# Expert weights of a fused decoder trunk: gate and up blocks loaded as one transfer each

## What is computed

```
def expert_block(args):
    xblk, e = args
    hid = jax.nn.silu(xblk @ w_gate[e]) * (xblk @ w_up[e])
    return hid @ w_down[e]
```

## Time and profile before

| | |
|---|---|
| median of three runs | 1823.66 us (1822.59 to 1826.57) |
| the profiled execution | 1824.36 us, of which the traced span is 1822.3 us |
| PE, DVE, ACT busy | 97%, 72%, 57% of the span |
| HBM read, written | 484.66 MB, 26.74 MB |
| expert loads | 3 x 128 DMAs of 1 MB, 10.9 to 11.7 us from issue to landing (medians) |

### The profile page before, as it was taken

One profiled execution on the slowest core, in us unless ns is written; L12 is line 12 of the kernel. 1 busy time (PEld: TensorE's weight loads), 2 busy tenths in 40 slices (PEclk: granted clock), 3 DMA queues, 4 the chain that ended last, 5 costly groups with the idle time before them and its releaser, 6 DMA issues.

```text
span 1822.3 us, 21866 instructions
## 1 busy us (share of the span) xinstructions
PE 1767.5 (97%) x7712; PEld 1183.5 (65%) x7719; DVE 1315.4 (72%) x1368; ACT 1030.0 (57%) x1067; POOL 227.2 (12%) x136
## 2 busy tenths in 40 slices
PE   8999998999999999999999999998999999999997
PEld 6876785566555555657787777877565555555564
DVE  4999757888778878864443533456878888888877
ACT  4225636777777777753221312233777777777774
POOL 0030001112221222100000000000021222221220
PEclk9999999999999999989999999999999999999999
DMA  8521046999999999994212221222899999999995
GB/s 281 185 93 47 13 176 242 402 409 402 404 400 397 394 399 397 395 368 153 83 57 93 93 93 46 93 93 93 316 408 408 408 401 398 407 402 398 400 389 232
DMA packets 101503, 494.95 MB, mean 272 GB/s; under 512 B 14153, under 2 KB 26441, under 8 KB 52160
## 3 DMA queue, kind: packets, MB, share of 16 engines
q1 hardware_dynamic: 88192, 467.69, 65.7%
q0 software_dynamic: 10176, 16.24, 2.7%
q10 hardware_dynamic: 3072, 10.18, 1.5%
HBM read 484.66 MB, written 26.74 MB: 281 GB/s over the span
## 4 chain that ended last, share of the span: by engine, by line
PE 51%; DMA 28%; DVE 12%; ACT 6%; issue 2%; SPq 1%; DVEq 0%; ACTq 0%
DMA raw<-in_expert_w_gate 28%; PE psum L901 8%; PE psum L902 8%; PE psum L903 8%; DVE w_lo L729 6%; ACT w_hi L742 5%; PE psum L1050 4%; PE psum L984 4%; PE psum L981 3%; PE psum L1434 2%; DVE xs L1918 2%; PE psum L1060 1%; PE psum L1065 1%; PE psum L1061 1%; PE psum L1002 1%
## 5 line engine op out<-in xcount | busy, mean ns | idle before, releaser
L729 DVE TENSOR_TENSOR w_lo<-raw,w_hi 128x2048 fp32r<-128x2048 f32 x320 | 731.5, 2288 | 181.5 <-ACT w_hi L742 175.3
L742 ACT ACTIVATE w_hi<-raw 128x2048 fp32r<-128x2048 f32 x320 | 610.8, 1912 | 229.0 <-DMA raw<-in_expert_w_up 116.5
L984 PE MATMUL psum<-w_lo,uT_hi 128*64 128x512 f32 x992 | 273.4, 397 | 5.8 <-DVE w_lo L729 2.3
L707 ACT ACTIVATE w_hi<-raw 128x2048 fp32r<-128x2048 f32 x46 | 88.0, 1914 | 329.7 <-PE psum L903 329.6
L981 PE MATMUL psum<-w_hi,uT_hi 128*128 128x512 f32 x868 | 248.7, 403 | 6.6 <-DVE uT_hi L2191 6.6
L715 DVE TENSOR_TENSOR w_lo<-raw,w_hi 128x2048 fp32r<-128x2048 f32 x46 | 105.4, 2291 | 200.2 <-ACT w_hi L707 200.2
L2521 POOL DMA_INDIRECT y_dram<-y_e,index x60 | 137.5, 2292 | 786.3 <-DVE y_e L2226 773.1
L1050 PE MATMUL psum<-raw,hidT_f 128*64 128x512 f32 (+1 forms) x496 | 226.1, 598 | 0.0
L984 PEld LDWEIGHTS psum<-w_lo,uT_hi 128*64 128x64 f32 x992 | 130.4, 135 | 103.6 <-DVE w_lo L729 26.9
L981 PEld LDWEIGHTS psum<-w_hi,uT_hi 128*128 128x128 f32 x868 | 161.6, 192 | 45.3 <-DVE uT_hi L2191 7.2
L2516 POOL DMA_INDIRECT x_e<-xs_dram,index x64 | 73.3, 1145 | 672.3 <-DVE index L2186 625.8
(11 more groups left out here) (267 smaller groups left out, 2348.6 us busy)
## 6 DMA issues: line engine op xcount, KB each, us to landing
raw<-in_expert_w_gate SPq DMA_DIRECT2D x128, 1024.0 KB, 11.5
raw<-in_expert_w_up SPq DMA_DIRECT2D x128, 1024.0 KB, 11.7
raw<-in_expert_w_down SPq DMA_DIRECT2D x128, 1024.0 KB, 10.9
raw<-in_odd_w_in SPq DMA_DIRECT2D x8, 2048.0 KB, 9.6
raw<-in_odd_w_in SPq DMA_DIRECT2D x8, 1024.0 KB, 7.9
raw<-in_odd_w_out SPq DMA_DIRECT2D x4, 2048.0 KB, 7.5
raw<-in_even_w_in SPq DMA_DIRECT2D x3, 2048.0 KB, 12.5
y_dram<-zeros SPq DMA_DIRECT2D x8, 512.0 KB, 12.5
```

The costliest lines, as they stand in the source:

```text
L729: nc.vector.tensor_tensor(part(w_lo[b]), src, part(w_hi[b]).bitcast(F32), ALU.subtract).then_inc(m.lo[b], 1)
L742: nc.scalar.activation(part(w_hi[b]), src, ACT.Copy).then_inc(m.hi[b], 1)
L984: mm = nc.tensor.matmul(psum[0:FIRST, bank], xeT_hi[:, 8 * b + 4 * half + j, 0:FIRST], lo[:, j], start=False, stop=False)
```

## The change

Gate and up blocks are loaded by one DMA each, with 16 KB in each partition, by the new function load_block. It waits for the second half of the slot only (the first half has been split by then, as DVE splits in order), and adds to `landed`. Down is loaded in halves as before. ACT waits for the whole block before it splits either half of gate or up. `front_at` now counts down blocks alone. Nothing is changed in what the engines compute or in their order.

```diff
+    def down_block(n):
+
+        k = n - moe_start[int(n >= moe_start[1])]
+        return k == n_moe - 1 or k >= 2 and (k - 2) % 3 == 2
+
...
         front_at[n] = 16 * sum(1 for e in list(range(moe_start[0], first_odd)) + list(range(moe_start[1], n + 1))
-                               if e <= n and e % SLOTS == n % SLOTS)
+                               if e <= n and e % SLOTS == n % SLOTS and down_block(e))
...
-                if raw_half:
+                if raw_half or not is_down(k):
                     eng.wait_ge(landed[n % SLOTS], landed_at[n] + 32 * turn)
                 else:
                     eng.wait_ge(front[n % SLOTS], front_at[n] + 32 * turn)
...
                         if s or kind != "down":
-                            for half in range(2):
-                                load_half(kind, number, x, turn, half)
+                            if kind == "down":
+                                for half in range(2):
+                                    load_half(kind, number, x, turn, half)
+                            else:
+                                load_block(kind, number, x, turn)
...
+                def load_block(kind, s, e, turn):
+
+                    src, number = {"gate": (wg_dram, gate_no), "up": (wu_dram, up_no)}[kind]
+                    n = first + number(s)
+                    freed(n - SLOTS, 1, turn)
+                    sp.dma_start(raw[:, n % SLOTS], one(src, layer, e)).then_inc(landed[n % SLOTS], 16)
```

## The result

| | before | after |
|---|---|---|
| median | 1823.12 us (1821.6 to 1827.03, six runs) | 1846.26 us (1838.07 to 1849.58, six runs) |
| ratio to before | | 1.0114, interval 1.0099 to 1.0129 |
| profiled execution | 1824.36 us | 1838.07 us, its fastest |

The changed kernel is slower by 1.1%. I had forecast no change. Some executions of any of these kernels run a few per cent slower throughout, at a lower clock; they are left out of all ratios. The profiled execution of after is 13.7 us longer than that of before, and this is the difference that the traces can explain.

What follows compares the result with a forecast made beforehand. The prediction took DMA as the full engine pacing the expert parts. A shorter stream, later start and later splits summed to -7.8 + 3.3 + 4.6 = +0.1 us, so no change: median 1823.8 us, range 1815 to 1834.

Steps and rivals of the forecast that it cites:

- What bounds the kernel: Expert parts: DMA is full from the start; PE waits each step for the last split of up and for `uT_lo`.
- Term 1: Weight load stream in the experts: 16 KB rows save 0.075 us a block over 52 blocks x 2 layers, -7.8 us.
- rival 2: Load queue: 16 KB rows are cut into two packets, so term 1 shrinks to 0.8 us; +7.1, 1831 us; chance 0.08.
- The faster stretches: Sign in the load stream: a stretch with gate and up alone should read about 428 GB/s.
- Term 2: Start of each layer's experts: first gate load goes out only when the whole block can, 2.3 us later; +3.3 us together.
- Term 3: PE's last wait in each layer: weights of a landed block are split 2.3 us later, +4.6 us together.
- Does the DMA stay fed?: Check on load issue in expert steps: each load goes out 2.6 us before the one ahead lands; all fits, narrowly.
- with 1.3 to spare: Gate load in an expert step: out 3.9 us before down's second half lands, 1.3 us beyond the 2.6 needed.
- The 2.6 us themselves: Lead a load needs: 5.1 us from issue to landing of a half in idle queues, of which 2.5 are data.
- Rival 1: Second layer, 26 steps: up issued too late, needing 3.5 us of lead, engines dry 0.4 us each; +10, 1834; chance 0.15.
- Rivals 3 and 4: Expert steps get shorter: long rows lessen the loss beside gathers, 1807 us, chance 0.12; or fewer transfers, 1795, chance 0.04.
- rival 4: Expert steps: each transfer holds the engines a fixed time; two fewer leave PE's 15.7 us pace; 1795 us; chance 0.04.

Runs made afterwards that it cites:

- e15: Kernel before, SP's loop written out, first gate load of each step held until down's first half landed; two runs, 1843.56 and 1850.71 us.
- e1: Kernel before with the changed kernel's late issue and late split of gate and up, but 8 KB rows; two runs, 1840.37 and 1845.73 us.
- after again: The changed kernel measured a second time, beside the follow-up runs; ratio 1.0068 to before, +12.4 us.
- e2: Kernel before, but ACT waits for the whole gate or up block before splitting, halves issued as before; ratio 1.0035 to before, +6.4 us.
- e3: Kernel before, but both halves of gate or up issued together when the second is free, split as they land; ratio 0.9982 to before, -3.3 us.
- e9: Changed kernel with gather and scatter of each expert step cut to one 4 KB row; ratio 1.0272 to before, +75 us to before with the same cut.
- e13: Control: kernel before with SP's loop over the steps written out, same loads, order and waits; 1827.24 us, ratio 1.0003 to before.
- e14: Kernel before, SP's loop written out, first gate load of each step held until the up block ahead landed; 1818.47 us, ratio 0.9952 to before.

## Why the prediction was wrong, point by point

- **What bounds the kernel.** Right: DMA with the waits of PE at the line that takes `uT_lo`.
- **Term 1, -7.8 us.** Its price was right, its arrival not. Packets of the load queue in 1320 to 1740 fell by a third, and they are of 16 KB, so rival 2 fell:

```profile
q1 hardware_dynamic: 14669, 160.80, 95.9%
```

  The same row of before has 22403 packets. A clean stretch, 1233.5 to 1237, has 79 packets of 16 KB beside 15 tiny ones; 86.4% x 3.5 us x 16 / 79 = 612 ns, against 618 to 624 expected and 2 x 309. But from the first gate load inside the experts to the one behind PE's last wait, the stream got 2.2 us longer in the first layer and 3.4 in the second, where 3.9 less were due in each. The steps are 16.45 us, not 16.05. The faster stretches, which I had named as a sign, are there (the best of 40 slices of 1320 to 1740 reads 427 GB/s, in before 423), but didn't show in the steps: the table above says why.
- **Term 2, +3.3 us.** Right. Against the time at which the second half of its buffer is free, the first gate load of the experts lands 2.8 us later in the first layer and 1.0 in the second, where its second half had been slow in before too (7.1 us from issue to landing, 5.7 in the first layer): 3.8 together. That the gathers would take some of it back is not shown.
- **Term 3, +4.6 us.** Right. At its last wait PE ran 2.5 us further behind the landings in either layer, 4.9 together. In one step the last split of up ended 6.5 us after the landing that ACT waited for, as forecast (times, DVE; ACT began at 1578.33):

```profile
1580.29 4.49 DVE L734 TENSOR_TENSOR w_lo<-raw,w_hi 128x2048 fp32r<-128x2048 f32 x2 [0.55 <-ACT w_hi L747]
```

- **"Does the DMA stay fed?"** This is the step that failed. It asked whether each load goes out 2.6 us before the one ahead has landed. It did: gate was out 3.6 to 3.9 us ahead, up 4.0. But it took the landings of the step as given, at the old pace, and so measured spare time against a point that the loads themselves move. The question was whether a buffer gets round in a step: 7.3 us from landing to split, which was right, plus SP's 0.4, which I had left out, plus the 7.9 us of a load into idle queues, 15.6 of the 16.05 that I had forecast for a step. My sentence "with 1.3 to spare" held for the lead and hid that under 0.5 us was left for the queue, of which a gate load took 0.86. The rows for it stood there: the earlier trace rows.
- **The 2.6 us themselves.** They came from one load into idle queues, and say when the first packets flow, not when the last of 16 engines has work. e15 cost three times what they give. The Trainium skill, page "DMA: Bandwidth & Descriptors", section "Why a DMA increments its semaphore by 16 and not by 1", says that the engines of a DMA finish independently and each adds its own 1. The trace agrees: those 16 come 5.1 us apart on average in before, and up to 8.3. A landing is the last engine's, and the others need their next work earlier.
- **Rivals.** Rival 1 named the right place and sign, at 1834 us; the median was 1846. By it the step would have gone from 16.2 to 16.6 us, and in the second layer only. In fact the first layer lost too, as its steps at 15.7 us were gone from the start: the loop binds PE-bound steps as well. Rivals 3 and 4 fell: no step got shorter. To rival 4, the fixed time per transfer: e1, with two transfers for each of after's, is 2 to 7 us slower than after again (two runs), where 32 us had been at stake.
- **The new sum.** In the profiled pair: +5.6 for the stream in place of -7.8, +3.8 and +4.9 for terms 2 and 3, and 2.9 us at the end of the first layer, where the last scatter landed later. Against that stands -3.4 before the first expert part, in work that the change doesn't touch. These are pieces of one shift, one behind the other, and make +13.8, as much as the two spans differ (1822.3 and 1836.1). The median of the six runs is 8 us above the profiled one; of this no trace tells.

## What to carry to other kernels

Before merging loads into bigger ones, go once round each buffer: issue to landing in idle queues, landing to the last reader, and the issue itself. If the sum comes near the step, every wait in the queue lengthens the step, however far ahead the load seems to go out. A merged load makes both parts of the loop longer at once, and either alone may be free (e2, e3) where the pair is not (e1). Where a queue is kept very full, try to hold one load back: at one place it was worth 9 us here, at all three it cost 7.

## What the hardware showed that I had not expected

- A load into idle queues reaches its first engine 0.95 to 1.0 us after the issue and its last of 16 after 1.8 to 2.3 us (16 expert loads of before and after). One that goes out while the load ahead is ending reached its last engines after 3.8 us (e9, above).
- First packets after a pause are slow when all engines start together: 0.64 to 2.04 us for 16 KB instead of 0.61 (e9, above). In e15 packets that took 0.4 to 0.8 us too long were 234 in 410 us, in e13 86, in e14 36.
- Less traffic beside the loads can make a kernel slower: after with one row in and out took 1873 us, with all its gathers 1839 (medians of e9 and of after again).
- The Trainium skill, the same page, section "Bandwidth", advises batches of 1 MiB and more. Going from 1 to 2 MB gained only the 7 ns for each pair of rows, and lost time in the loop; no run here speaks on smaller ones.
